# Row maximum of the attention scores in the same vector operation as the bias add, bias made on GpSimd, and GpSimd's state decay behind VectorE's state-column operations

## The reference, cut to what matters

```python
dist = (q_pos[:, None] - k_pos[None, :]).astype(jnp.float32)
bias = jnp.where(dist >= 0, -slopes[:, None, None] * dist, -jnp.inf)
s1 = jnp.einsum('bqhd,bkhd->bhqk', q1, k1).astype(jnp.float32) * scale + bias
s2 = jnp.einsum('bqhd,bkhd->bhqk', q2, k2).astype(jnp.float32) * scale + bias
attn = jax.nn.softmax(s1, axis=-1) - lam * jax.nn.softmax(s2, axis=-1)
```

```python
S = S * jnp.exp(g_t)[..., None, None]
u = v_t - jnp.einsum('bhk,bhkv->bhv', k_t, S)
S = S + jnp.einsum('bhk,bhv->bhkv', k_t * b_t[..., None], u)
o = jnp.einsum('bhk,bhkv->bhv', q_t, S)
```

## Time and profile before

| | us |
|---|---|
| median of three runs (lowest, highest) | 2824.42 (2824.34, 2824.59) |
| profiled execution | 2825.48 |
| its span | 2823.7 |
| PE busy / DVE busy / ACT busy / POOL busy | 2742.1 / 1390.5 / 1020.0 / 228.8 |
| mean granted clock of PE, of full speed | 0.986 |

### The profile page before, as it was taken

How to read it: one execution, slowest core, us unless ns; L and a number is a source line. 1 busy time by engine, 2 the same in 40 slices (tenths; PEclk the granted TensorE clock), 3 DMA queues, 4 the chain that set the end, 5 groups by cost and what they waited for, 6 DMA issues and landing times.

```text
span 2823.7 us, 56788 instructions
## 1 busy us (share of the span) xinstructions
PE 2742.1 (97%) x23882; PEld 2591.7 (92%) x23882; DVE 1390.5 (49%) x1628; ACT 1020.0 (36%) x1151; POOL 228.8 (8%) x140
## 2 busy tenths in 40 slices
PE   7999999998899999999999999999998999999997
PEld 7999999965499999999999999999655999999997
DVE  5333346735666543333643333557356665333336
ACT  5333224312463433322344332333125533344222
POOL 0111001221000011100001100012300000111000
PEclk9999999998999999999999999999989999999998
DMA  4222232276522222222322222323764222222221
GB/s 143 97 96 71 92 131 91 82 214 205 154 98 90 91 90 96 92 82 86 105 90 89 89 78 91 131 92 110 218 205 139 88 90 93 89 89 80 93 90 67
DMA packets 119393, 304.61 MB, mean 108 GB/s; under 512 B 14930, under 2 KB 24914, under 8 KB 118738
## 3 DMA queue, kind: packets, MB, share of 16 engines
q1 hardware_dynamic: 119250, 302.57, 33.2%
HBM read 291.08 MB, written 11.44 MB: 107 GB/s over the span
## 4 chain that ended last, share of the span: by engine, by line
PE 91%; DVE 4%; DVEq 2%; ACT 2%; issue 1%; POOL 0%; DMA 0%; SPq 0%; POOLq 0%; ACTq 0%
PE ps L603 68%; PE ps L651 12%; PE ps L815 2%; PE ps L903 1%; DVE mx L1926 1%; ACT sc L1207 1%; PE ps L969 1%; DVEq L1925 1%; PE ps L884 1%; PE ps L702 1%; PE ps L870 1%; PE ps L1120 0%; DVEq L1735 0%; DVE sc L1922 0%; PE ps L733 0%
## 5 line engine op out<-in xcount | busy, mean ns | idle before, releaser
L603 PE MATMUL ps<-Hh,whi 128*128 128x260 f32 x3456 | 696.3, 283 | 17.1 <-DVE Hl L1662 13.8
L603 PE MATMUL ps<-Hl,whi 128*128 128x260 f32 x3456 | 694.5, 282 | 0.0
L603 PE MATMUL ps<-Hh,wlo 128*128 128x260 f32 x3456 | 693.3, 282 | 0.0
L1207 ACT ACTIVATE whi<-raw 128x2048 fp32r<-128x2048 f32 (+2 forms) x225 | 395.9, 1760 | 780.6 <-PE ps L603 670.5
L1596 DVE TENSOR_TENSOR wlo<-raw,whi 128x2048 fp32r<-128x2048 f32 (+2 forms) x213 | 444.2, 2085 | 291.2 <-ACT whi L1207 291.1
L603 PEld LDWEIGHTS ps<-Hh,whi 128*128 128x128 f32 x3456 | 531.9, 189 | 18.1 <-issue 16.7
L603 PEld LDWEIGHTS ps<-Hl,whi 128*128 128x128 f32 x3456 | 533.9, 189 | 0.0
L603 PEld LDWEIGHTS ps<-Hh,wlo 128*128 128x128 f32 x3456 | 532.9, 189 | 0.0
L1207 ACT ACT_TABLE_LOAD x163 | 209.1, 1283 | 303.2 <-PE ps L603 233.7
L1596 DVE TENSOR_TENSOR ta<-ps,R 128x520 f32<-128x520 f32 x88 | 61.6, 700 | 476.3 <-PE ps L603 475.2
L603 PE MATMUL ps<-Gh,whi 128*128 128x260 f32 x1408 | 284.0, 283 | 0.0
(11 more groups left out here) (271 smaller groups left out, 3002.2 us busy)
## 6 DMA issues: line engine op xcount, KB each, us to landing
raw<-in_ffn_up SPq DMA_DIRECT2D x176, 512.0 KB, 4.3
raw<-in_ffn_down SPq DMA_DIRECT2D x128, 352.0 KB, 3.2
kb<-in_cache_k SPq DMA_DIRECT2D x128, 256.0 KB, 3.1
kb<-in_cache_v SPq DMA_DIRECT2D x128, 256.0 KB, 3.0
raw<-in_w_in SPq DMA_DIRECT2D x56, 512.0 KB, 4.5
raw<-in_w_gate SPq DMA_DIRECT2D x32, 512.0 KB, 4.8
raw<-in_w_ab SPq DMA_DIRECT2D x16, 512.0 KB, 4.2
raw<-in_w_o SPq DMA_DIRECT2D x16, 512.0 KB, 4.4
```

Source lines behind the costliest of these rows:

```text
L603: last = nc.tensor.matmul(ps[:, bank + 2 * m + c, 0:HT], w, x[:, k0 + k, c * HT:(c + 1) * HT], start=starts and k == 0 and n == 0, stop=st ...
L1207: return nc.scalar.activation(out, in_, func, **kw)
```

## The change

1. `att_max` no longer adds the bias and reduces in three instructions. It calls `tensor_tensor_reduce` once per map, which adds a ready bias tile to the scores, writes `sc`, and gives the row maximum as an accumulator output. The `reduce_max` and one `drain` go.
2. The bias of a head (distance times slope, 128x512) is made by POOL, one `tensor_scalar` per head, in two tiles by turns. Heads 0 and 1 follow the DVE copy `kc1`; heads 2 and 3 wait for the last `nm` of the head whose tile they take.
3. `decay(b)` on POOL waits for a new step `x{b}` of DVE, the end of `state_new(b)`, in place of PE's reads.
4. PE's list: `state_turn(0)` and `state_outer(0, 0)` stand later in level 1, `key(10)` stands ahead of `state_read(1, 1)`.

```diff
@@ PE, levels
                     key((None, 4, 7, 9, 12, 15)[l])
-                    if l == 1:
-                        state_turn(0)
-                    elif l == 2:
+                    if l == 2:
                         state_outer(0, 2)
...
                     invert_low(l, 1)
                     if l == 1:
+                        state_turn(0)
+                        key(5)
                         state_outer(0, 0)
-                        key(5)
...
                     elif l == 3:
+                        key(10)
                         state_read(1, 1)
-                        key(10)
@@ POOL
                 def decay(b):
-                    pool.wait_ge(s_pe.sem, s_pe.at(f"r{b}", L))
+                    pool.wait_ge(s_dve.sem, s_dve.at(f"x{b}", L))
...
                 nc.gpsimd.memset(Pz[:, :, :], 0.0).then_inc(q_pool.on("pz", L), 1)
+                for h in range(H):
+                    if h > 1:
+                        pool.wait_ge(a_dve.sem, a_dve.at(f"max{h - 2}3", L))
+                    elif h == 0:
+                        pool.wait_ge(d_dve.sem, d_dve.at("kc1", L))
+                    nc.gpsimd.tensor_scalar(bias[h % 2][:, :], CM[:, M_DIST:M_DIST + SEQ], CC[:, C_SLOPE + h:C_SLOPE + h + 1], None, ALU.mult
+                                            ).then_inc(a_pool.on(f"b{h}", L), 1)
@@ DVE
-                    TT(U[:, 8:12, SEQ + 4 * b:SEQ + 4 * b + 4], ocol[:, :, :].rearrange("p s h -> p h s"), aq[:, :, 0:4], ALU.add)
+                    TT(U[:, 8:12, SEQ + 4 * b:SEQ + 4 * b + 4], ocol[:, :, :].rearrange("p s h -> p h s"), aq[:, :, 0:4], ALU.add
+                       ).then_inc(s_dve.on(f"x{b}", L), 1)
...
+                    if q == 0:
+                        dve.wait_ge(a_pool.sem, a_pool.at(f"b{h}", L))
                     for m in range(2):
-                        V.scalar_tensor_tensor(out=sc[:, q % 2, m, 0:n], in0=CM[:, M_DIST + SEQ - n:M_DIST + SEQ],
-                                               scalar=CC[:, C_SLOPE + h:C_SLOPE + h + 1],
-                                               in1=ps[:, 4 + m, 0:n], op0=ALU.mult, op1=ALU.add)
-                    dve.drain()
-                    V.reduce_max(mx[:, q % 2, :], sc[:, q % 2, :, 0:n], AXX)
+                        V.tensor_tensor_reduce(out=sc[:, q % 2, m, 0:n], in0=bias[h % 2][:, SEQ - n:SEQ], in1=ps[:, 4 + m, 0:n],
+                                               scale=1.0, scalar=NEG, op0=ALU.add, op1=ALU.max, accum_out=mx[:, q % 2, m:m + 1])
                     dve.drain()
```

## The result

The changed kernel takes **2784.9 us** (median of 4 runs, 2779.9 to 2788.1), the kernel before 2824.4 beside it: ratio 0.986, 95% interval 0.9843 to 0.9877. The profiled execution took 2784.7 with a span of 2782.9, mean granted clock 0.993.

The account below looks back on a forecast made before the run. PE, busy 97% of the span, bounds the kernel; only its stalls and lower clock can be won. Terms -9.1 (A), -1.3 (B), -13.7 (C), +3.0 (D) sum to -21.1, from the 2824.4 median to 2803.3 us, range 2794 to 2816.

Parts of the forecast that it names:

- A, the stall: Inversion part, batch 1: PE's stall before the low matmuls of level 4, group 1 goes, 2.93 us per layer.
- B: Inversion part, batch 0: PE's waits at the state columns and `Uz` shrink by 0.65 us per layer, 1.3 in all.
- A, the clock: Behind the level 4 stall PE's clock no longer falls: 1.25 us gained in layer 0, 1.98 in layer 1.
- C: Attention part, fused maximum: DVE gives up 2.80 us per head, PE 1.7, so 13.7 in all; bounds 8.8 to 16.8.
- (1): Attention head, q3: DVE's 1.10 us brings `sc` forward and closes PE's 0.86 us stall, with 0.24 left over.
- (2): Attention head, transposes of the values waiting for ACT and q0's maximum: 0.5 us of PE's stall goes.
- (3): Attention head, q1: DVE's 0.57 us ends in its own wait for PE before `vn`, so nothing is gained.
- (4): Attention head, q2: of DVE's 0.83 us only 0.35 is gained, since `S` needs PE's matmuls.
- D: Seam, bias on POOL: holds DVE's small coefficient operations and delays `Co`, a loss of 1.5 us per layer, +3.0.
- R1: Rival: the fused operation takes two cycles per element, so C gains nothing and the time is 2817; chance 0.13.
- R2: Rival: each fused call has a fixed price, slower from 0.57 us, 2852 us at a price of 1.0; chance 0.07.
- R3: Rival: PE only trades its stalls and the clock falls behind A as before, 2813 us; chance 0.12.

Follow-up runs that it names:

- e3: The kernel before with only the decay's wait changed to the state-column step, PE's list as before: 2808.8 us.
- e1: The kernel before with the decay's new wait and the moves in PE's list, no fused maximum and no bias on POOL: 2809.8 us.
- e2: The changed kernel with the decay waiting for PE's reads and PE's list in the old order, so fused maximum and POOL bias alone: 2798.3 us.
- e13: The kernel before with 4 and 3 unread matmuls on constants filling two stalls of every head, at q2 and q3: 2820.7 us.
- e12: The changed kernel with DVE's coefficients ahead of the last state addition and kc1 copy, and first item's scores ahead of the first scan product: 2784.1 us.
- e4: The kernel before with only the moves in PE's list, the decay waiting for PE's reads as before: 2821.7 us.

## Why the prediction was wrong, point by point

The forecast was 2803.3 us in a range of 2794 to 2816; 2784.9 was measured. From the profiled execution of before, the changed one came 19.7 us lower than forecast: 16.1 in PE's busy time and 3.6 in its idle time. The step that failed is the last of the sum: that PE's clock "also falls at two other places of the stage, whose phase a shift may change by some 3 us". The profile before has more of them, four or five stretches at the lower level per layer beside the one behind the stall (in layer 0 at 636, 670 to 685, 749 and 769 to 777). The changed kernel has 20 us at the lower level instead of 61. By the estimate above that is about 16 us of time, where the forecast had 3.2 for the place behind the stall and, for all the others, 3 either way. Some 3 us more of busy time went with the shorter heads at full clock, for which the forecast had nothing.

- **A, the stall**: right, 2.93 us per layer gone, and by the wait alone (`e3`). **B**: right in size, 0.67 of 0.65, but the cover by PE's list was not needed for it (`e3`). The 6.0 us of the table are less than 7.2 because PE, now earlier, waits 0.80 us per layer for `kc1` at the end of the part, where it waited 0.34 before.
- **A, the clock**: right at its place. The falls behind the stall are gone, and they stood behind seven of eight such stalls. What it left out is every other fall of the inversion part, above all the one at 636 that goes with batch 0's wait. Busy time in the inversion part fell by 8.2 us and not 3.2. And a fall is not bound to a stall just in front (`e1`).
- **C**: the step "the fused operation itself I take like the old one" and the reads at 0.10 were both too dear. DVE gives up 4.1 us per head, not 2.80: 3.60, and eight calls that are 0.06 shorter, with reads at nothing. DVE's busy time in `e2` says the same without the drains, 29.9 / 8 = 3.74. Of PE's stalls in a head 2.4 us go and not 1.7: (1) 0.86 gone as forecast, (2) 1.07 instead of 0.5, (3) nothing as forecast, (4) 0.50 instead of 0.35. Over both layers the six whole heads give up 14.2 us of idle time and the items around them 2.6, together the 16.8 of the table. That 16.8 is also the forecast's bound for free reads is luck. With 8.1 us of busy time the part gained 24.9, over the 18 that the prediction had named as its sign of being wrong.
- **D**: +3.0 forecast; the hold is 0.4 per layer. `cf <- cf, ls`, put down as held, took 0.29 us against 0.16 alone; `Co` took 0.51 against 0.24. The forecast took the first for held and the second not; the rows show the larger hold on the second. PE's busy time in the seam falls by more than its idle time grows (2.9 against 0.9).
- **The sum**: with all idle terms at their measured size it is 2825.5 - 21.9 - 3.2 = 2800.4, inside the range. The idle terms that were mis-sized, C by 3.1 and D by 2.1, with 1.2 the other way in A and B, would not have taken it out. PE's busy time did.
- **Rivals**: R1 is dead, 682 ns. R2's mechanism is real, a dose on the call does lengthen a head, but its price is not there, and that its point came out (0.58 against 0.57) is luck. R3's stalls did not come back.

The Trainium skill (SBUF — State Buffer, Who interferes with whom) would have a DVE instruction with two SBUF inputs wait for a whole POOL instruction that reads SBUF; that holds for `ucol` before (3.35 us beside the decay, 0.18 without), and not for `cf` beside the bias, 0.29 us. The measurement decides for this pair; why they differ was not tried. The Trainium skill (TensorE: Matmul & The Clock Gate, Why this matters for your kernels) ties a fall to idle gaps between bursts of matmuls. The falls behind the stall of 2.93 us agree. `e13` agrees in kind, though the stalls that it filled were of about 1 us. `e1` shows a fall without a gap.

What stays open: what brings the clock down where PE hardly stands still, at the end of the inversion part and in the seam above all, and how batch 0's wait would act on a fall some 25 us behind it. In every profile but one (layer 0 of `e12`) there is a fall between 660 and 685 us and its twin in layer 1.

## What to carry to other kernels

When stalls go from a stretch in which the granted clock is below 1, count the clock for the whole stretch and not for the place behind the stall: here about 16 of 39 us came that way, an estimated 0.4 us for each us at the lower level. A maximum folded into a float32 addition on DVE with one input in PSUM costs nothing over the addition. What a longer or shorter step of such a loop is worth is found by following each stall to the step that feeds it; a dose on the step then gives the slack (here about 1.15 us of a head). Before a POOL instruction is started by a semaphore, look which two-input DVE operations stand next to it: one wait was worth 14 us (`e3`).

## What the runs showed of the hardware that was not expected

- The fused operation with its accumulator takes 682 ns for 512 elements (one input in PSUM), the plain addition 680, multiply and add 742; its accumulator read of 83 ns lies wholly beside other operations.
- PE's granted clock fell with PE busy throughout (`e1`, 614 to 661) and once held behind a stall of 2.93 us (layer 0 of `e4`), though behind seven of eight such stalls it was lower. Two profiles of the same changed kernel have 20 and 31 us at the lower level.
- Filling stalls with matmuls that nobody reads made the kernel before faster, by 4.0 us in 2824.7 with an interval of 1 to 7 (`e13`).
- `Co` is recorded as 0.51 us beside the bias, but the next DVE operation starts 0.15 us after its start: PE, which waits for its end, is held, DVE's list is not.
